# Up-projection of a squared-relu MLP: two matmuls of 512 and 256 columns per weight block become three of 256 columns

## The reference, cut to what matters

```python
def squared_relu_mlp(xn, w_up, w_down):          # w_up 1024 x 4096, w_down 4096 x 1024
    return jnp.square(jax.nn.relu(xn @ w_up)) @ w_down

f = squared_relu_mlp(rms_norm(h, norm_gains[i, 2]), ffn_w_up[i], ffn_w_down[i])
h = h + rms_norm(f, norm_gains[i, 3])
```

## Time and profile before

| | |
|---|---|
| Time, median of 3 runs | 1737.17 us (1736.73 to 1737.23) |
| Span of the profiled execution, first to last instruction | 1734.4 us |
| PE (TensorE matmul) busy | 1721.4 us, 99% of the span |
| PEld (TensorE weight load) busy | 1424.5 us, 82% |
| DVE busy | 1183.7 us, 68% |
| ACT busy | 1040.8 us, 60% |
| POOL busy | 144.5 us, 8% |
| Granted TensorE clock, mean | 1.000 |

### The profile page before, as it was taken

The page is one execution under the profiler, slowest core; times in us unless marked ns, Lnnn a source line. Parts: engine busy times, 40 slices in busy tenths (PEclk is TensorE's granted clock), DMA queues, the critical chain, the costliest instruction groups (busy, mean ns, idle before and its releaser), DMA issues. The chain is left out here.

```text
span 1734.4 us, 22528 instructions
## 1 busy us (share of the span) xinstructions
PE 1721.4 (99%) x8559; PEld 1424.5 (82%) x8559; DVE 1183.7 (68%) x1677; ACT 1040.8 (60%) x1657; POOL 144.5 (8%) x121
## 2 busy tenths in 40 slices
PE   8999999999999999999999999999999999999998
PEld 7888887788888877888888888888888888788887
DVE  6756567677666778766667766588776666786664
ACT  7755567757565766654475744477664446665442
POOL 0000011200000010211000101002011100102110
PEclk9999999999999999999999999999999999999999
DMA  8545454255554533555554555454455545335552
GB/s 323 203 181 197 151 213 146 98 195 200 189 194 161 215 122 122 206 194 184 181 187 169 218 182 191 170 206 147 158 205 185 184 181 193 127 116 222 183 190 73
DMA packets 44987, 310.55 MB, mean 179 GB/s; under 512 B 5232, under 2 KB 5616, under 8 KB 8400
## 3 DMA queue, kind: packets, MB, share of 16 engines
q1 hardware_dynamic: 44464, 307.96, 48.5%
q0 software_dynamic: 272, 1.05, 0.2%
q10 hardware_dynamic: 144, 0.11, 0.0%
HBM read 308.05 MB, written 1.05 MB: 178 GB/s over the span
## 5 line engine op out<-in xcount | busy, mean ns | idle before, releaser
L1286 DVE SCALAR_TENSOR_TENSOR wlo<-raw,first,whi 128x512 fp32r<-128x512 f32 x704 | 501.8, 775 | 120.2 <-ACT whi L695 119.6
L695 ACT ACTIVATE whi<-raw,first 128x512 fp32r<-128x512 f32 x704 | 450.1, 714 | 104.8 <-PE ps L2117 84.2
L2115 PE MATMUL ps<-whi,xs 128*128 128x512 f32 (+1 forms) x1184 | 472.7, 399 | 1.1 <-DVE wlo L1286 0.9
L2117 PE MATMUL ps<-whi,xs 128*128 128x512 f32 (+1 forms) x1184 | 461.0, 389 | 0.0
L2116 PE MATMUL ps<-wlo,xs 128*128 128x512 f32 (+1 forms) x1184 | 460.0, 388 | 0.0
L1283 DVE TENSOR_TENSOR wlo<-raw,whi 128x2048 fp32r<-128x2048 f32 x110 | 251.7, 2307 | 68.5 <-ACT whi L690 68.3
L2115 PE MATMUL ps<-whi,hhi 128*128 128x512 f32 x720 | 282.4, 392 | 0.0
L2117 PE MATMUL ps<-whi,hlo 128*128 128x512 f32 x720 | 280.6, 390 | 0.0
L2116 PE MATMUL ps<-wlo,hhi 128*128 128x512 f32 x720 | 280.4, 389 | 0.0
L2204 PE MATMUL ps<-xs,whi 128*128 128x512 f32 x768 | 273.0, 399 | 0.0
L2115 PEld LDWEIGHTS ps<-whi,xs 128*128 128x128 f32 x1184 | 222.4, 188 | 48.9 <-issue 3.9
(11 more groups left out here) (235 smaller groups left out, 1306.4 us busy)
## 6 DMA issues: line engine op xcount, KB each, us to landing
raw<-in_w_parts SPq DMA_DIRECT2D x285, 1024.0 KB, 4.8
gain<-in_gains SPq DMA_DIRECT2D x10, 512.0 KB, 6.3
x<-in_x SPq DMA_DIRECT2D x2, 512.0 KB, 6.4
raw<-in_w_parts SPq DMA_DIRECT2D x2, 512.0 KB, 5.8
arena<-in_bias_line POOLq DMA_DIRECT2D x1, 1024.0 KB, 11.9
out<-x SPq DMA_DIRECT2D x4, 256.0 KB, 2.1
const<-in_const_in SPq DMA_DIRECT2D x1, 288.0 KB, 13.1
wup<-in_gla_up SPq DMA_DIRECT2D x1, 192.0 KB, 12.4
```

The lines of the kernel that those rows point to most:

```text
L695: nc.scalar.activation(whi[n % HIS][:, cols], raw[n % LOS][:, cols], ACT.Copy, scale=gcol[:, COLUMNS[n] + kk:COLUMNS[n] + kk + 1]).then_in ...
L1286: nc.vector.scalar_tensor_tensor(out=lo[:, cols], in0=whole[:, cols], scalar=gcol[:, COLUMNS[n] + kk:COLUMNS[n] + kk + 1], in1=hi[:, cols] ...
L2115: nc.tensor.matmul(out_ap, a_hi, wh, start=first, stop=False)
L2117: return nc.tensor.matmul(out_ap, a_lo, wh, start=False, stop=last)
```

## The change

The product with `xlo` is accumulated onto the same 256 columns as the other two. The second half of the bank is no longer used, and with it go the copy on ACT and the addition on DVE; relu reads PSUM, and the banks come free with relu (`trelu_ready`).

```diff
-        def turned_banks(u, lower):
-            return ps[:, 4 + 2 * u:6 + 2 * u, SEQ * lower:SEQ * (lower + 1)]
+        def turned_banks(u):
+            return ps[:, 4 + 2 * u:6 + 2 * u, 0:SEQ]
...
-                def turned_copy(i, u):
-                    act.wait_ge(job_done, s["n_job"] + nth_job(i, u))
-                    if i >= 3:
-                        act.wait_ge(trelu_ready, turned_count(s, i - 1, u))
-                    nc.scalar.activation(LOWER[u], turned_banks(u, 1), ACT.Copy).then_inc(tcopy_ready, 1)
...
-                        for u in range(2):
-                            turned_copy(i, u)
...
-                def turned_sum(i, u):
-                    dve.wait_ge(tcopy_ready, turned_count(s, i, u))
-                    nc.vector.tensor_tensor(LOWER[u], turned_banks(u, 0), LOWER[u], ALU.add).then_inc(tsum_ready, 1)
...
                 def turned_relu(i, u):
-                    dve.wait_ge(tsum_ready, turned_count(s, i, u))
+                    dve.wait_ge(job_done, s["n_job"] + nth_job(i, u))
...
-                    nc.vector.scalar_tensor_tensor(out=R[:, u, :].rearrange("p (m n) -> p m n", m=2), in0=LOWER[u], scalar=0.0,
+                    nc.vector.scalar_tensor_tensor(out=R[:, u, :].rearrange("p (m n) -> p m n", m=2), in0=turned_banks(u), scalar=0.0,
...
-                            turned_sum(i, u)
                             turned_relu(i, u)
...
-                        pe.wait_ge(tsum_ready, turned_count(s, i - 1, u))
+                        pe.wait_ge(trelu_ready, turned_count(s, i - 1, u))
...
-                            nc.tensor.matmul(ps[:, 4 + m, :], whi[n % HIS][:, cols], xs[:, k, :, :].rearrange("p h n -> p (h n)"),
-                                             start=(k == 0), stop=False)
+                            nc.tensor.matmul(ps[:, 4 + m, 0:SEQ], whi[n % HIS][:, cols], xhi[:, k, :], start=(k == 0), stop=False)
+                            nc.tensor.matmul(ps[:, 4 + m, 0:SEQ], whi[n % HIS][:, cols], xlo[:, k, :], start=False, stop=False)
                             ins = nc.tensor.matmul(ps[:, 4 + m, 0:SEQ], wlo[n % LOS][:, cols], xhi[:, k, :], start=False,
                                                    stop=(k == KT - 1))
```

More of the change, by code:

```diff
@@ L372, in build @@
         HLO_T = hlo[:].rearrange("p t k n -> p k t n")
-        LOWER = [arena[:, 4096 + BANK * u:4096 + BANK * (u + 1)].rearrange("p (m n) -> p m n", m=2) for u in range(2)]
         def acc_tile(t):
@@ L421, in build @@
         row_ready = sem("row_ready")
-        tcopy_ready = sem("tcopy_ready")
-        tsum_ready = sem("tsum_ready")
         trelu_ready = sem("trelu_ready")
```

## The result

The changed kernel takes 1742.32 us (median, 1742.17 to 1742.61, 6 runs), the kernel before 1737.18 us. The ratio is 1.0031 (95% interval 1.0021 to 1.0040): 5.1 us slower. The forecast was 1742.7 us, and 0.60 for slower.

A forecast was written before the change was run, and what follows sets the result against it. The prediction took PE's matmul stream as the bound. 768 triples added 5.5 us to the 1734.4 us span, giving 1739.9, all else nothing; with 2.8 us from span to median, 1742.7 us, range 1736 to 1753.

The forecast's parts named there:

- Point 1: Turned up-product steps on PE: three 256-column matmuls take 360 ns against 352.8 for the pair, +5.5 us over 768 triples.
- the three sources for 120 ns: Earlier-trace paces of 512, 328 and 256 columns, agreeing on 12 to 14 ns overhead per matmul; the 256s were nearest.
- The 2.8 us between span and median: Amount by which the median of the runs exceeds the profiled span, added to the predicted span of 1739.9 us.
- Point 2: Second load of the same `whi` block in a triple: not skipped, already counted in the matmul sum.
- Point 3: Accumulating onto the same 256 columns every 120 ns: taken as nothing, +247 us if each sum waited for the one before.
- Points 4 and 5: Evacuation: removing ACT's copy (28.7 us) and DVE's addition (33.2 us) gains nothing; relu from PSUM stays at 0.69 us.
- Point 6: PE's wait for banks now hangs on relu, which may be some 10 us late; PE loses at most 0.9 us.
- Rival A: PE's triples run at the low end, at most 119.1 ns a matmul: no change within 3.5 us; chance 0.33.
- Rival B: Loads and matmuls disturb each other when all are short: 123 to 126 ns a matmul, 1749.6 to 1755.9 us; chance 0.15.
- Rival C: Loads pace PE's stream, columns fully overlapped: at most 116.1 ns a matmul; at 113 ns -10.6 us, 1726.6 us; chance 0.07.
- Rival D: In PE's triples a load is not hidden, +79 us, 1816 us, or the dependent sum waits, costing more; chance 0.03.
- The rule of the Trainium skill: A weight load overlaps a running matmul only on different row groups; 768 added loads would then cost an estimated 82 us.

The follow-up runs named there:

- e2_no_copy: Changed kernel with the old 512- and 256-column matmuls back, still without copy and addition, second bank half computed but unused: 1737.13 us, 1.0001 of the kernel before.
- e1_halves: Kernel before with its 512-column matmul cut into two of 256 writing the two bank halves, copy and addition kept: 1742.51 us, ratio 1.0032.
- e4_interleaved: Changed kernel with two groups' six matmuls reordered so no two running share a weight block or bank: 1742.75 us, 1.0032 of the kernel before.
- e6_cols128: Changed kernel with each matmul of a triple 128 columns wide except in the first slice, so work is missing: 1725.00 us, one execution.

## Why the prediction was right

- *The bound.* PE's stream, from its waits and not from its busy share alone: confirmed by e2_no_copy, in which 62 us less work on ACT and DVE moved the time by 0.01%.
- *Point 1, the matmuls.* The term was a triple at 360 ns against 352.8, +5.5 us. Measured are 120 ns a matmul and +0.23 us in each of the 20 unbroken steps. The first turned steps, one in each layer, lose 0.3 us each, as many of their pairs had run at 346.7 ns. Together the trace has +5.6 us in the 24 steps; e1_halves gives +5.5 us in its median with nothing but the matmuls changed. The nearest of the three sources for 120 ns, is weaker than it looked: read to the nanosecond, the trace has starts 119, 119 and 117 ns apart there, 118.3 on average, which would have spoken for no change. The 12 to 14 ns of overhead in the runs of 512 and 328 columns were the better source, and they held.
- *A term that I missed.* The down product behind a step became 0.04 us shorter (10.907 us against 10.943) in 16 of 20 cases, some -0.6 us. Before, the first 512s behind such a step started up to 241 ns apart rather than 227; now there is less of this. With the +5.6 us and small differences elsewhere this makes the 4.9 us from the first turned step on.
- *The 2.8 us between span and median* are no fixed difference. In every execution whose span is on record the time is 2.0 to 2.2 us above its own span, so the profiled execution of the kernel before (1734.4 us) was some 0.7 us faster than the median. The changed kernel's profiled execution took 1742.54 us, 0.2 above its median. That is why the spans differ by 6.1 us and the medians by 5.1. The medians' 5.1 us agree with the 4.9 behind the first stretch; how much of the 1.2 us ahead of it the other executions have, no run shows.
- *Point 2, the repeated load.* It was counted as a load like any other, and it is one: e4_interleaved never loads the same block twice in a row and keeps the pace.
- *Point 3, the sum onto fresh columns.* Taken at nothing, and nothing it is: e1_halves and e4_interleaved remove it each in its own way, and both stay at 120 ns.
- *Points 4 and 5.* Copy and addition at no gain, relu at 0.69 us from PSUM as from SBUF: as forecast. ACT lost 23.9 us of busy time and not 28.7, DVE 30.9 and not 33.2; busy time is a union of records that overlap (the sums of the records differ by 29.0 and 31.9 us), and nothing hangs on it.
- *Point 6, the wait for the banks.* No such wait is in the profile. ACT now splits the next weights inside the step (6.17 us busy where it was 4.21) rather than under the down product (3.83 for 6.78), as the prediction said it could; nothing came of it.
- *Rival A* was alive to the last: it needed 119.1 ns a matmul. The decision between "same" and "slower" hung on one nanosecond, and the 5.1 us measured are only 1.6 above the 3.5. The earlier trace rows could be read to 3 ns only, and the full reading lay on A's side. So the mechanism was foreseen, and that the change came out on this side of the bound was in part luck.
- *Rival B* assumed that loads and matmuls disturb each other more as more matmuls are short. It is the other way round: in a stream of one width the excess is gone. The half of the excess I gave it had no basis.
- *Rival C* needed a matmul of at most 116.1 ns, and the 120 measured refute it: the overhead of 12 to 14 ns does not vanish. Its part on loads was half right, there is a pace of loads (112 ns, e6_cols128), but it lies below the pace of 256 columns and doesn't bind here. The 102.5 ns that the prediction read for transposes is too low: the 512 behind them starts 28 ns after the last one, and the twelve themselves start 109 ns apart (1.20 us over eleven intervals).
- *Rival D* is refuted as well: 768 more loads cost 5.1 us and not 79, so a load is hidden, down to that floor. The rule of the Trainium skill that the prediction sets beside this rival stands in the page's section "The mechanism".

The Trainium skill, "TensorE: Matmul & The Clock Gate", section "LDWEIGHTS (loading the stationary operand)", gives columns by 1.2 GHz, an estimated 107 ns for 128. The runs show 112 as the pace of a matmul with its load, so the page is near. The Trainium skill's section "Back-to-back issue gap" on the same page has some 81 ns for a stream of loads and matmuls at 128 columns; with the operands of this kernel 128 columns cost 112 (e6_cols128), and the measurement decides here.

What stays open is the mechanism of the 6 ns a pair: why the successor of a 512 behind a 256 starts late, why it takes several matmuls to fade, and why the same alternation ran without it at the start of each layer. The runs show that the order changes its size in the unbroken steps, and no more.

## What to carry to other kernels

On a kernel whose PE stream has no waits, count matmuls and not only columns: one more matmul costs its fixed 13 ns even if its columns were streamed before, and removing work elsewhere pays nothing. (Here the triple cost only 7 ns more than the pair, since the pair carried an excess of 6.) Read a pace from first and last start over a counted stretch; differences of a few ns by a few hundred instructions are the whole effect here. And where long and short matmuls alternate and a pair costs more than the two paces together, try to group them first: two by two gave -4.5 us for a change of order alone.

## What was unexpected about the hardware

- A 256-column fp32r matmul with its own 128-column load runs at 120 ns, one of 192 or 128 columns at 112, the pace at which the loads start: between 128 and 192 columns the width is free.
- A pair of 512 and 256 columns takes 352.8 ns when the two alternate, 348.1 two by two, 348.4 eight by eight (11.15 us a step, by the same view), and 346.7 for most pairs at the start of the first turned step of a layer before, with the same instructions in the same alternation.
- Every kernel here with the 768 additional matmuls began 0.5 us later in its profile (PE's wait for the first DMA 5.3 or 5.4 us against 4.8). Why, and whether the other executions do so too, no run here shows.
